# Row sums of a conditioning matrix: multiply on GpSimd and sum on ScalarE instead of one fused operation on VectorE

## The reference, cut to what matters

```
cs = jax.nn.silu(c)                       # c: 1 x 1024
mod = cs @ w_ada + b_ada                  # w_ada: 1024 x 6144
sh1, sc1, gt1, sh2, sc2, gt2 = split(mod, 6)
h = rmsnorm(x, norm1_g) * (1.0 + sc1) + sh1
```

## Time and profile before

| | |
|---|---|
| three runs | 1395.16, 1398.03, 1398.88 us; median 1398.03 |
| the profiled execution | 1397.73 us, of which the span is 1395.9 |
| PE busy | 1335.7 us, 96% |
| DVE busy | 1040.9 us, 75% |
| ACT busy | 750.2 us, 54% |
| POOL busy | 42.4 us, 3% |
| granted clock of TensorE, mean | 0.995 of full speed |

### The profile page before, as it was taken

How to read it: one execution, slowest core, us unless ns; L and a number is a source line. 1 busy time by engine, 2 the same in 40 slices (tenths; PEclk the granted TensorE clock), 3 DMA queues, 4 the chain that set the end, 5 groups by cost and what they waited for, 6 DMA issues and landing times.

```text
span 1395.9 us, 22643 instructions
## 1 busy us (share of the span) xinstructions
PE 1335.7 (96%) x8944; PEld 1192.3 (85%) x8944; DVE 1040.9 (75%) x1786; ACT 750.2 (54%) x1164; POOL 42.4 (3%) x80
## 2 busy tenths in 40 slices
PE   7999999999999999999999999999979997999998
PEld 6899998898888879999998988888768886878886
DVE  4387667786778784776586776787778888688887
ACT  5354756545444444546657354444457776655553
POOL 1000000000000000000000000000010000000000
PEclk9999999999999999999999999999999999999999
DMA  9965444364677655444443655776624513345551
GB/s 267 215 236 191 179 151 161 137 218 179 244 273 273 249 211 180 168 155 165 143 172 121 230 193 204 272 271 247 226 91 167 211 62 121 109 178 184 194 195 61
DMA packets 42147, 262.00 MB, mean 188 GB/s; under 512 B 5229, under 2 KB 5613, under 8 KB 14782
## 3 DMA queue, kind: packets, MB, share of 16 engines
q1 hardware_dynamic: 32688, 227.28, 45.9%
q0 software_dynamic: 9264, 33.24, 7.3%
q10 hardware_dynamic: 94, 0.07, 0.0%
HBM read 258.99 MB, written 1.58 MB: 187 GB/s over the span
## 4 chain that ended last, share of the span: by engine, by line
PE 75%; DVE 14%; ACT 4%; DMA 4%; issue 3%; SPq 0%; DVEq 0%; ACTq 0%
PE psum L676 16%; PE psum L678 16%; PE psum L677 16%; PE psum L708 14%; PE psum L711 6%; DVE split L1723 5%; DMA ring<-stream 3%; ACT split L1241 1%; DVE arena L1716 1%; PE psum L810 1%; PE psum L940 1%; DVE arena L1889 1%; PE psum L707 1%; DVE feed L1723 1%; PE psum L823 1%
## 5 line engine op out<-in xcount | busy, mean ns | idle before, releaser
L1723 DVE TENSOR_TENSOR split<-ring,split 128x1024 fp32r<-128x1024 f32 x408 | 482.8, 1221 | 133.9 <-ACT split L1241 132.9
L1241 ACT CAST split<-ring 128x1024 fp32r<-128x1024 f32 x407 | 407.8, 1049 | 186.6 <-PE psum L678 162.7
L708 PE MATMUL psum<-h,split 128*128 128x512 f32 x960 | 335.3, 398 | 3.7 <-DVE split L1723 3.7
L676 PE MATMUL psum<-h,split 128*128 128x256 f32 x1088 | 311.2, 286 | 8.3 <-DVE split L1723 8.3
L677 PE MATMUL psum<-h,split 128*128 128x256 f32 x1088 | 307.7, 283 | 0.0
L678 PE MATMUL psum<-h,split 128*128 128x256 f32 x1088 | 307.7, 283 | 0.0
L711 PE MATMUL psum<-h,split 128*128 128x256 f32 x840 | 235.6, 280 | 0.0
L676 PEld LDWEIGHTS psum<-h,split 128*128 128x128 f32 x1088 | 208.5, 192 | 18.3 <-issue 14.8
L678 PEld LDWEIGHTS psum<-h,split 128*128 128x128 f32 x1088 | 208.6, 192 | 0.0
L677 PEld LDWEIGHTS psum<-h,split 128*128 128x128 f32 x1088 | 208.5, 192 | 0.0
L708 PEld LDWEIGHTS psum<-h,split 128*128 128x128 f32 x960 | 174.6, 188 | 39.3 <-issue 5.7
(11 more groups left out here) (344 smaller groups left out, 1925.9 us busy)
## 6 DMA issues: line engine op xcount, KB each, us to landing
ring<-stream SPq DMA_DIRECT2D x213, 1024.0 KB, 4.9
arena<-ada POOLq DMA_DIRECT2D x48, 512.0 KB, 5.3
arena<-bias_by_distance POOLq DMA_DIRECT2D x8, 384.0 KB, 30.9
gain<-norm_rows POOLq DMA_DIRECT2D x4, 512.0 KB, 7.4
x<-x_in SPq DMA_DIRECT2D x2, 512.0 KB, 4.7
ring<-stream SPq DMA_DIRECT2D x2, 512.0 KB, 8.1
gain<-mod_rows POOLq DMA_DIRECT2D x2, 512.0 KB, 6.2
out<-x SPq DMA_DIRECT2D x4, 256.0 KB, 2.0
```

The costliest lines, as they stand in the source:

```text
L676: pe.matmul(out_, a[0], b[0], start=first, stop=False)
L708: mm = pe.matmul(bank[b + m].rearrange("p (a t) -> p a t", a=2), high, h[:, :, k, :], start=k == 0, stop=k == KT - 1)
L1241: act.copy(split_of(x)[:, 0, n], ring[:, AT[x] % RING, n]).then_inc(wh_ready, 1)
L1723: return dve.tensor_tensor(out_, value, high.bitcast(F32), ALU.subtract)
```

## The change

The fused VectorE instruction of each tile is taken away. GpSimd multiplies the tile by `c_row` in place once it has landed (`ada_scale`), and signals `ada_scaled`; ScalarE, at the end of the same job in its own list, copies the tile onto itself with the sum over the row as the second output, and signals `ada_summed`. GpSimd's program interleaves the two: the load of tile a, then the product of tile a-1.

```diff
+        ada_scaled = sem("ada_scaled")
...
+            def ada_scale(a):
+                pool.wait_ge(ada_loaded[a % 2], (a // 2 + 1) * 16)
+                pool.tensor_tensor(ada_ring[:, a % 2, :], ada_ring[:, a % 2, :], c_row, ALU.mult).then_inc(ada_scaled, 1)
+
             for a in range(NADA):
...
                 if a >= 2:
                     pool.wait_ge(ada_summed, a - 1)
                 pool.dma_start(ada_ring[:, a % 2, :], ada[a]).then_inc(ada_loaded[a % 2], 16)
+                if a:
+                    ada_scale(a - 1)
+            ada_scale(NADA - 1)
...
+                    if k in ADA_AT:
+
+                        a = ADA_AT[k]
+                        act.wait_ge(ada_scaled, l * ADA_L + a + 1)
+                        act.activation(ada_ring[:, a % 2, :], ada_ring[:, a % 2, :], ACT.Copy, accum_out=mod_l[:, a:a + 1]) \
+                            .then_inc(ada_summed, 1)
...
-                    if k in ADA_AT:
-
-                        a = ADA_AT[k]
-                        dve.wait_ge(ada_loaded[a % 2], (l * (ADA_L // 2) + a // 2 + 1) * 16)
-                        w = ada_ring[:, a % 2, :]
-                        dve.scalar_tensor_tensor(w, w, 1.0, c_row, ALU.mult, ALU.mult, accum_out=mod_l[:, a:a + 1]) \
-                            .then_inc(ada_summed, 1)
```

## The result

The changed kernel takes 1402.37 us (median of 9 runs, 1398.77 to 1408.16); the kernel before took 1395.63 in the 9 runs beside it. The ratio is 1.0040 with a 95% interval of 1.0021 to 1.0059. It is slower, by a little more than can be told from no change. A second series, further down, gave 1.0079 (1.0058 to 1.0101).

The account below looks back on a forecast made before the run. It took TensorE to bound the kernel, with at most 7.3 us of waits to win. Regular rounds 0, ScalarE 0, after gate 5 +0.7, end of layer 0 +0.1 gave +0.8 on 1397.73: 1398.5 us, range 1394.0 to 1412.0.

Parts of the forecast that it names:

- The likeliest case: Whole time within 0.3% (4.2 us) of the kernel before, held or not, 1395.8 to 1398.5 us; chance 0.55.
- Rival 1: In all 18 regular rounds the product holds the low parts beyond their 0.81 us slack: 1404 to 1412 us; chance 0.23.
- rival 2: Second product gets ahead of the second low part; TensorE waits 1.3 us in 18 rounds: 24 us, 1422; chance 0.13.
- Off VectorE: 48 fused instructions removed return 55 us to VectorE; value 0 in regular rounds, 0.97 us a layer after gate 5.
- Onto ScalarE: 48 sums of 1.05 us, 50 us over all, fit ScalarE's idle time or are hidden; price 0.
- signs that I had named for being wrong: Products over 3 us, TensorE waiting for a low part in each round, or ScalarE found waiting for GpSimd.
- Onto GpSimd: 48 two-operand products of 128x1024, taken as 2.4 us each, between bounds of 0.95 and 2.86; no sum waits for them.
- Held instructions: VectorE's two-input subtractions stand still for the product's whole rest; hidden in regular rounds, +0.7 after gate 5, +0.1 ending layer 0.
- The wait behind gate 5: TensorE's 0.97 us wait there: 0.33 us a layer lost to the product's holding instead of 0.97 won.
- The wait at the end of layer 0: TensorE's 1.89 us wait there stays, and the product's holding of 0.14 us has no slack: +0.1.
- The step that failed: Regular rounds: second product from 393.26 waits for the second low part, holds the next pair by 1.35 us, hidden.
- rival 3: Faster: no holding and some of 7.3 us of waits shrink, 1395.8, 1391 at best; over 4.2 us faster: chance 0.09.

Follow-up runs that it names:

- run 1: The changed kernel without GpSimd's products, ScalarE summing the tiles as loaded: 1395.11 us, ratio 0.9984 to the kernel before.
- run 7: The kernel before with the fused VectorE instruction of gate 5 moved behind the first wt job: 1392.68 us, ratio 0.9957.
- run 11: The kernel before with gate 5's tile moved behind the first wt job, measured again: 1396.5 us, ratio 0.9979.
- run 2: The changed kernel with products on GpSimd but the sums on VectorE instead of ScalarE: 1421.7 us, ratio 1.0172 to the kernel before.
- run 6: The changed kernel with four GpSimd MEMSETs of the tile in place of each product: 1393.62 us, ratio 0.9975 to the kernel before.
- run 10: The changed kernel again without an edit, for more times and a second profile: 1408.78 us, ratio 1.0079 to the kernel before.
- run 5: The changed kernel with each product made twice on GpSimd: 1492.5 us, ratio 1.068 to the kernel before.
- run 4: The changed kernel with both products of an FFN round placed together after the low part following gate's start: 1400.2 us, ratio 1.0015 to the kernel before.

## Why the prediction was right in most steps, and where it failed

**The time** of 1398.5 us is 3.9 us under the measured 1402.4, and the range of 1394 to 1412 holds it. The likeliest case, within 0.3% of the kernel before, did not come: it is 0.4% and 0.8% slower in two series, which I had given 36% (rivals 1 and 2). That the time is so near is partly luck: the rise was forecast as 0.8 us and is 6.7 by the medians, and 2.1 us of the difference are hidden because the profiled execution from which I started was that much slower than the median of the nine runs. Rival 1, the larger part of the 36%, did not come at all: the products last 2.4 us and no regular round waits for the first low part. What came is rival 2, in a few rounds and not in all.

**Off VectorE: right.** In regular rounds the removed instruction only became waiting: the idle time in front of the second addition of `up` grew from 0.65 to 1.80 us, as computed.

```profile
388.05 0.69 DVE L1989 TENSOR_TENSOR arena<-psum,arena 128x512 f32<-128x512 f32 x1 [1.80 <-ACT arena L1363]
388.77 0.81 DVE L1991 TENSOR_TENSOR arena<-arena 128x512 f32<-128x512 f32 x1
```

That 0.97 us a layer could be won behind gate 5 and no more in the FFN is shown by runs 1, 7 and 11.

**Onto ScalarE: right.** 50.5 us more (750.2 to 800.7) against 50, and hidden (run 1). One thing was missed, and it is one of the signs that I had named for being wrong: the sum behind `up 5` waits 1.0 us for its product, twice in all. ScalarE still had 0.68 us of idle time behind it, so it cost nothing.

**Onto GpSimd: right.** A product alone takes 2.39 to 2.43 us, taken as 2.4. Its mean of 2.71 holds the times in which GpSimd waits for VectorE.

**Held instructions: right in kind and in size.** Their places were right but for the one step below. L1991 was to be held by 0.14 us in a regular round; it took 0.81 to 0.89 instead of 0.69. The wait behind gate 5 was to be 0.97 + 0.33 = 1.30; it is 1.26:

```profile
422.87 2.12 DVE L1991 TENSOR_TENSOR arena<-arena 128x512 f32<-128x512 f32 x1
...
422.02 2.42 POOL L622 TENSOR_TENSOR arena<-arena 128x1024 f32<-128x1024 f32 x1
...
427.46 0.47 PE L717 MATMUL psum<-h,split 128*128 128x512 f32 x1 [1.26 <-DVE split L1738]
```

The wait at the end of layer 0 was to be 1.89 + 0.14 = 2.03; it is 2.08. The rule of the Trainium skill ("SBUF — State Buffer", Who interferes with whom), by which two-input instructions of VectorE contend with GpSimd instructions that read SBUF and not with those that only write, is what runs 2 and 6 show here: a multiplication of 0.69 us takes 1.91 beside a product and 0.69 beside MEMSETs.

**The step that failed** is "it waits until 394.46 and ends at 396.86 ... Hidden too": the second product of a round was taken to come behind the second low part in every round, and its getting ahead was made a rival of all rounds or none, at 24 us and 13%. The product was taken to start behind its load, at 393.26, the data having landed "mostly by then" by the median of 5.3 us. In the changed kernel landings are spread wider,

```profile
DMA to landing us min/median/max: 3.6/5.8/8.1
```

and those of the second products of regular rounds come 5.7 us after the issue or later. So in most rounds the landing and not the load sets the start, at or behind the border of the two low parts, and each round comes out by itself. In the two profiles of the changed kernel the product got ahead in one regular round of layer 0 and one of layer 1, and in none and three. In four of these five it started 0.07 to 0.08 us after its data had landed; in the fifth (859.36 in run 10) they had landed 0.34 us earlier and it started as the load ahead of it ended. Each time TensorE waited 1.2 us, near the 1.3 that rival 2 had computed, and the stretch grew by 1.5 to 1.6 (the matmuls of 0.39 us there otherwise start 0.23 us apart, and don't overlap across a wait). With the +0.8 us forecast (0.29, 0.28 and 0.19 us came in the first profile), two and three such rounds at 1.5 give +3.8 and +5.3; the two profiles' FFN stretches together are 4.0 and 5.3 us over those of the kernel before in the same series. That the landings decide was read from these two profiles; no run moved them on purpose.

One sum is off as well: "1391 at best" in rival 3 is 1397.73 - 7.3 = 1390.4. Nothing rests on it.

**What else adds** is open in part. By the medians the changed kernel is 6.7 and 9.2 us slower in the two series, so 2.7 and 3.9 us lie outside what the FFN stretches show. The profiled executions of the changed kernel are faster than the medians of their series (by 3.6 and 2.4 us), so other executions may have more rounds of the dear kind; only the two were profiled. The clock is a second candidate. The wait of 2.08 us at the end of layer 0 is 0.19 us longer than that of before, and in the first profile of the changed kernel it was followed by a stretch of 3.4 us at 1.2 GHz:

```profile
508.22 0.39 PE L687 MATMUL psum<-split,feed 128*128 128x512 f32 x1
510.69 0.49 PE L685 MATMUL psum<-split,feed 128*128 128x512 f32 x1 [2.08 <-DVE split L1738]
511.00 0.61 PE L686 MATMUL psum<-split,feed 128*128 128x512 f32 x1
511.40 0.63 PE L687 MATMUL psum<-split,feed 128*128 128x512 f32 x1
```

The same matmul takes 0.39 us before the wait and 0.63 behind it. From 510.69 to the next fixed place it took 199.5 us, and 197.9 before: 1.6 us. In the second profile it didn't happen (198.1), so this is a risk and not a constant part. The mean clock over the runs is nearly the same in both kernels (0.9912 and 0.9919 in the second series), and I can't put a number on it for the median. A third is chance: at the border to the second block a CAST of VectorE stood still for 1.1 us beside the six MEMSETs in one profile of each kernel and for 3.00 in the other.

## What to carry to other kernels

Before moving work off an engine, find the waits of the bottleneck that the moved instructions stand in front of: here it was 0.97 us twice out of 55 us of relief, and moving one tile won it without any second engine. A GpSimd product of two SBUF operands is not free for VectorE, even off every path: place it where VectorE idles or has one input in PSUM (L1989 kept its 0.69 us beside the product), by a wait on what VectorE has just finished. Where two engines reach for the same thing within a few hundredths of a microsecond, price each round by itself: here the landing of a transfer put one or the other first. A median over transfers of two kinds hides this; take the landings of the very transfers in question.

## What the runs showed of the hardware that I had not expected

- Who holds whom can change at the border of two instructions that stand back to back: the product above was wanted while the first low part ran, and went ahead of the second, although that was next in VectorE's queue. In the regular rounds of the two profiles of the changed kernel, the four products recorded 0.11 to 0.16 us before the end of the first low part went ahead, and the ten recorded 0.03 to 0.10 before it came behind the second; the fifth that went ahead is recorded 0.02 us after that end. Six MEMSETs in a row let a waiting CAST go on early (1.1 us) or only when all were done (3.00 us), and both kernels show both.
- The holding is mutual. Products that started beside a subtraction and had to wait for it took up to 3.5 us instead of 2.4.
- The CAST of 128x512, one input from SBUF, is held by GpSimd's product (2.51 instead of 0.43 us, run 5) and by its MEMSET; the two-input instructions only by the product.
- TensorE's clock fell to half in stretches of 3.4 or 6.8 us (10.2 at times in runs 5 and 6), in most cases around one of its own longer waits. With a wait of 1.89 us at the end of layer 0 the clock stayed whole in eight of nine profiles (all but run 4). At the wait of 3.2 us at the end of layer 1 it fell in all eleven profiles that have that wait, between 1.2 us before the wait's end and 1.4 us behind it.
